# The last expert's down projection in quarters of the output columns, with the second block's first weight chunk between its second and third quarter

## What is computed

```python
xs = jax.vmap(lambda hb, ib: hb[ib])(h, idx)             # 64 tokens per expert
a = jnp.einsum('becd,edf->becf', xs, w_gate)             # 1024 -> 2048
u = jnp.einsum('becd,edf->becf', xs, w_up)
y = jnp.einsum('becf,efd->becd', jax.nn.silu(a) * u, w_down)   # 2048 -> 1024
y = (y * gate[..., None]).astype(h.dtype)
out = jax.ops.segment_sum(y.reshape(-1, dm), seg, num_segments=bn * seq)
...
x = x + out;  x = rms_norm(x, final_g)                   # end of the first block
u = rms_norm_2(h, norm1_gain[l]);  proj = u @ w_in[l]    # start of the second
```

## Time and profile before

| | us |
|---|---|
| median of 3 runs (lowest, highest) | 1888.03 (1887.39, 1888.33) |
| the profiled execution, by the same clock as the runs | 1889.88 |
| its span in the trace | 1888.1 |
| PE busy | 1737.5 (92%) |
| DVE busy | 668.1 (35%) |
| ACT busy | 443.6 (23%) |
| 16 DMA engines, share of the span | 64.5% |

### The profile page before, as it was taken

The page is one execution under the profiler, slowest core; times in us unless marked ns, Lnnn a source line. Parts: engine busy times, 40 slices in busy tenths (PEclk is TensorE's granted clock), DMA queues, the critical chain, the costliest instruction groups (busy, mean ns, idle before and its releaser), DMA issues. The chain is left out here.

```text
span 1888.1 us, 19429 instructions
## 1 busy us (share of the span) xinstructions
PE 1737.5 (92%) x8120; PEld 1038.7 (55%) x8120; DVE 668.1 (35%) x903; ACT 443.6 (23%) x546; POOL 0.2 (0%) x4
## 2 busy tenths in 40 slices
PE   6999996999897997979979799799999999999997
PEld 5888874343342432324323243257767788888885
DVE  7886533101010010101101001057645475645654
ACT  4534322110010100101000010065333343423332
POOL 0000000000000000000000000000000000000000
PEclk9999997999999999999999999999999999999999
DMA  5235436999999999999999999950402223222311
GB/s 183 82 91 174 161 140 250 400 428 428 427 428 428 430 428 428 428 429 428 429 428 428 428 427 428 427 195 1 178 27 87 88 89 112 89 89 89 111 45 44
DMA packets 76389, 492.47 MB, mean 261 GB/s; under 512 B 7472, under 2 KB 12592, under 8 KB 51504
## 3 DMA queue, kind: packets, MB, share of 16 engines
q1 hardware_dynamic: 76336, 491.71, 64.5%
HBM read 487.49 MB, written 2.10 MB: 259 GB/s over the span
## 5 line engine op out<-in xcount | busy, mean ns | idle before, releaser
L1182 PE MATMUL ps<-xs,xe 128*64 128x512 f32 x2048 | 461.5, 598 | 66.6 <-DMA xs<-w_up 35.3
L1182 PEld LDWEIGHTS ps<-xs,xe 128*64 128x64 f32 x2048 | 141.7, 137 | 379.1 <-issue 264.6
L1194 PE MATMUL ps<-xs,hidT 128*64 128x512 f32 x1024 | 229.8, 596 | 13.9 <-DMA xs<-w_down 9.2
L412 DVE TENSOR_TENSOR lo<-raw,hi 128x2048 fp32r<-128x2048 f32 (+1 forms) x73 | 164.8, 2258 | 174.6 <-ACT hi L403 171.4
L1409 DVE TENSOR_TENSOR hid<-hid,ps 128x512 f32<-128x512 f32 x32 | 20.6, 684 | 524.1 <-PE ps L1182 524.1
L403 ACT ACTIVATE hi<-raw 128x2048 fp32r<-128x2048 f32 (+1 forms) x73 | 138.0, 1890 | 218.5 <-PE ps L466 98.5
L466 PE MATMUL ps<-xh,hi 128*128 128x512 f32 x416 | 165.2, 397 | 0.8 <-DVE ga L931 0.8
L466 PE MATMUL ps<-xl,hi 128*128 128x512 f32 x416 | 162.2, 390 | 0.0
L1194 PEld LDWEIGHTS ps<-xs,hidT 128*64 128x64 f32 x1024 | 73.9, 136 | 148.2 <-issue 127.1
L442 PE MATMUL ps<-xh,hi 128*128 128x512 f32 x384 | 150.2, 391 | 1.1 <-DVE xt L1915 0.9
L442 PE MATMUL ps<-xl,hi 128*128 128x512 f32 x384 | 149.4, 389 | 0.0
(11 more groups left out here) (415 smaller groups left out, 1782.4 us busy)
## 6 DMA issues: line engine op xcount, KB each, us to landing
xs<-w_up SPq DMA_DIRECT2D x64, 2048.0 KB, 32.8
xs<-w_gate SPq DMA_DIRECT2D x64, 2048.0 KB, 32.0
xs<-w_down SPq DMA_DIRECT2D x64, 2048.0 KB, 31.3
raw<-w_in SPq DMA_DIRECT2D x25, 1024.0 KB, 6.7
raw<-ffn_up_w SPq DMA_DIRECT2D x24, 1024.0 KB, 5.1
raw<-ffn_down_w SPq DMA_DIRECT2D x12, 1024.0 KB, 5.1
raw<-w_out SPq DMA_DIRECT2D x8, 1024.0 KB, 5.0
xin<-x_t SPq DMA_DIRECT2D x4, 512.0 KB, 8.0
```

Source lines behind the costliest of these rows:

```text
L412: dve.tensor_tensor(lo[slot][:, 0:size], raw[:, raw_slot(n), 0:size], hi[slot][:, 0:size].bitcast(F32), ALU.subtract).then_inc(sem("lo_don ...
L1182: mm = pe.matmul(ps[64 * half:64 * half + 64, bank + b, :], xe[:, k, CAP * u:CAP * (u + 1)], xs[n % NXS][:, f:f + 512], start=(k == 0), st ...
L1194: mm = pe.matmul(ps[64 * nn:64 * nn + 64, YB, :], hidT[:, 4 * (c % 2) + kk, CAP * half:CAP * (half + 1)], xs[n % NXS][:, kk * D + nn * 512 ...
```

## The change

The host lays out the last expert's `w_down` a second time, as `w_down_q`: quarter q holds all 2048 rows and the columns 256q to 256q+255. It is still 2 MB a quarter. The last expert's down projection then runs quarter by quarter (`down_by_columns`): 32 matmuls of 128x64 by 128 columns each, into banks 4 and 7 in turn. After each quarter ACT copies 256 columns of `yy`, so two tiles of `xt` can be scattered (`last_scatter`, through two banks instead of three). PE's order becomes: quarters 0 and 1, tiles 0 to 3 scattered, chunk N2 multiplied, quarters 2 and 3, tiles 4 to 7 scattered, sums of squares, chunk N2+1. SP issues chunk N2's load ahead of quarters 2 and 3. ACT and DVE follow: the work on tiles 0 to 3 comes before that on tiles 4 to 7, and DVE now makes `lo` of chunk N2 behind the first four adds and `lo` of N2+1 behind all eight low parts. Quarters 2 and 3 have new places in memory, since `xh` and `xl` of tiles 0 to 3 are now written before they are used; `ivc` and `cur` move for the same reason.

```diff
+        "w_down_q": i["w_down"][0][NE - 1].reshape(4, P, 4, 4, 256).transpose(1, 3, 0, 2, 4).reshape(P, 4, XCH),
...
-        ivc = at("ivc", [P, 2, NE], F32, B + 60.5)
-        cur = at("cur", [P, 2, 2], F32, B + 60.75)
+        ivc = at("ivc", [P, 2, NE], F32, B + 55.5)
+        cur = at("cur", [P, 2, 2], F32, B + 55.75)
...
+        x67 = at("x67", [P, 2, XCH], F32, 64)
+        xq3 = at("xq3", [P, XCH], F32, B + 73)
+        last_home = (xs[4][:], xs[5][:], x67[:, :, XCH // 2:], xq3[:])
...
+            def down_by_columns(i):
+                pe.wait_ge(sem("hidT_done"), i * 4 + 4)
+                for q in range(4):
+                    n = NX - 4 + q
+                    x_arrived(pe, n, 0)
+                    if q >= 2:
+                        pe.wait_ge(sem("yy_done"), YLAST + 2 * (q - 1))
+                    home = last_home[q]
+                    for c in range(4):
+                        for kk in range(4):
+                            f = 256 * (4 * c + kk)
+                            for nn in range(2):
...
+                                mm = pe.matmul(ps[64 * nn:64 * nn + 64, last_bank(q), 0:P],
+                                               hidT[:, 4 * (c % 2) + kk, CAP * (c // 2):CAP * (c // 2 + 1)], wv,
+                                               start=(c == 0 and kk == 0), stop=(c == 3 and kk == 3))
+                    mm.then_inc(sem("xs_used"), 1)
+                    if q == 1:
+                        last_scatter(0)
+                        last_scatter(1)
+                        chunk_mms(pe, N2, PP, 0, 4, xh, xl, closes=False, by_tile=("xl_done", KD + 1))
+                last_scatter(2)
+                last_scatter(3)
+            def last_scatter(q):
+                if q == 0:
+                    pe.wait_ge(sem("t1_done"), NE // 2 + 1)
+                pe.wait_ge(sem("yy_done"), YLAST + 2 * (q + 1))
+                for m in (2 * q, 2 * q + 1):
+                    if m >= 2:
+                        pe.wait_ge(sem("sc_taken"), KD * (NE // 2) + m)
+                    pe.matmul(ps[:, TB + m % 2, :], yy[:, m * P:(m + 1) * P], t1[:], start=True, stop=True) \
+                        .then_inc(sem("sc_ps"), 1)
...
-                        act.wait_ge(sem("xs_used"), NX - 4)
-                        make_hi(act, NEXP)
+                        for q in range(4):
+                            act.wait_ge(sem("xs_used"), NX - 3 + q)
+                            for nn in range(2):
+                                o = 64 * nn
+                                a(yy[64:P, 256 * q + 128 * nn:256 * q + 128 * nn + 128], ps[o:o + 64, last_bank(q), 0:P], ACT.Copy,
+                                  scale=cur[o:o + 64, 1, 1:2]).then_inc(sem("yy_done"), 1)
+                            if q == 1:
+                                make_hi(act, NEXP)
+                                for m in range(4):
+                                    new_tile(act, m)
+                        break
...
+            for m in range(4):
+                add_last(m)
             make_lo(dve, NEXP)
...
+            for m in range(4):
+                new_rest(m)
+            for m in range(4, KD):
+                add_last(m)
+            for m in range(4, KD):
+                new_rest(m)
             make_lo(dve, NEXP + 1)
...
-            chunk_mms(pe, N2, PP, 0, 4, xh, xl, closes=False, by_tile=("xl_done", KD + 1))
...
+            for m in range(4, KD):
+                new_tile(act, m)
+                if m == 5:
                     make_hi(act, NEXP + 1)
...
-            for n in range(NX - 16, NX):
+            for n in range(NX - 16, NX - 4):
                 load_x(n)
-            for j in range(4):
+            for q in range(4):
+                n = NX - 4 + q
+                if q == 2:
+                    sp.wait_ge(sem("xs_used"), NX - NXS + NEXP % NRAW // 2 + 1)
+                    load_chunk(sp, NEXP)
+                sp.wait_ge(sem("xs_used"), min(n - NXS + 1, NX - NXS) if q < 2 else NX - NXS)
+                src = w["w_down_q"][:, q, :]
+                d(last_home[q], src.rearrange("p (a b) -> p a b", a=2) if q == 2 else src).then_inc(x_sem(n % NXS), 16)
+            for j in range(1, 4):
```

More of the change, by code:

```diff
@@ L1160, in rest_of_indices, with last_bank @@
             mm.then_inc(sem("idb_ps"), 1)
+        YLAST = 4 * (NE // 2 - 1) + 3
+        def last_bank(q):
+            return (YB, TB + 2)[q % 2]
         def experts_pe(pe):
@@ L1224, in pair @@
                     pe.wait_ge(sem("yy_done"), i * 4 + (2 * u + 1))
+                    if u == 1 and last:
+                        down_by_columns(i)
+                        break
                     for c in range(4):
@@ L1235, in pair @@
                                 gather(pe, k)
+            def down_by_columns(i):
[10 more added lines that the diff above has]
+                            for nn in range(2):
+                                wv = home[:, f // 2048, f % 2048 + 128 * nn:f % 2048 + 128 * nn + 128] if q == 2 else \
+                                    home[:, f + 128 * nn:f + 128 * nn + 128]
+                                mm = pe.matmul(ps[64 * nn:64 * nn + 64, last_bank(q), 0:P],
[17 more added lines that the diff above has]
+                        .then_inc(sem("sc_ps"), 1)
             pair(0, first=True)
@@ L1240, in experts_pe @@
             pair(NE // 2 - 1, last=True)
-            for q in range(4):
-                scatter(pe, NE // 2, q)
         def experts_act(act, a):
@@ L1414, in experts_dve, with new_rest, add_last, new_tile @@
             pair(NE // 2 - 1, last=True)
-            make_lo(dve, NEXP)
[L1416 to L1424, removed]
+            stt = dve.scalar_tensor_tensor
+            def new_rest(m):
+                dve.wait_ge(sem("xh_done"), KD + m + 1)
+                stt(xl[:, m, :], xt[:, m, :], gxx[:, m:m + 1], xh[:, m, :].bitcast(F32), ALU.mult, ALU.subtract) \
+                    .then_inc(sem("xl_done"), 1)
+            def add_last(m):
+                dve.wait_ge(sem("sc_ps"), KD * (NE // 2) + m + 1)
+                tt(xt[:, m, :], xt[:, m, :], ps[:, TB + m % 2, :], ALU.add).then_inc(sem("sc_taken"), 1)
+            for m in range(4):
+                add_last(m)
+            make_lo(dve, NEXP)
+            for m in range(4):
[4 more added lines that the diff above has]
+                new_rest(m)
             make_lo(dve, NEXP + 1)
         N2, SCS = NEXP, 1 + KD * (NE // 2 + 1)
+        def new_tile(act, m):
+            act.wait_ge(sem("sc_taken"), SCS - KD + m + 1)
+            act.activation(xh[:, m, :], xt[:, m, :], ACT.Copy, scale=gxx[:, m:m + 1]).then_inc(sem("xh_done"), 1)
+            for j, g in enumerate((None, gss)):
+                act.activation(squared(j, m), xt[:, m, :], ACT.Square, scale=1.0 if g is None else g[:, m:m + 1]) \
+                    .then_inc(sem("nrm_sq"), 1)
         def squared(j, k):
@@ L1433, in second_pe @@
         def second_pe(pe):
-            chunk_mms(pe, N2, PP, 0, 4, xh, xl, closes=False, by_tile=("xl_done", KD + 1))
-            pe.wait_ge(sem("yy_done"), 4 * (NE // 2) + 1)
+            pe.wait_ge(sem("yy_done"), YLAST + 8)
             for k in range(KD):
@@ L1602, in second_act @@
         def second_act(act, a):
-            for m in range(KD):
-                if m == 4:
+            for m in range(4, KD):
+                new_tile(act, m)
+                if m == 5:
                     make_hi(act, NEXP + 1)
[L1607 to L1611, removed]
             make_hi(act, N2 + 2)
```

## The result

The changed kernel takes 1891.07 us (median of 20 runs, 1887.74 to 1893.98) against 1888.52 for the kernel before in the same session (1885.57 to 1890.59): ratio 1.0013, 95% interval [1.0007, 1.0019], so +2.5 us, between +1.3 and +3.6. By the bound of the prediction, 0.2%, that is the same; forecast were +2.2 us and 1890.2. The profiled execution has a span of 1892.1 us, 4.0 more than the one before, and the traces say where these 4.0 are.

The account below looks back on a forecast made before the run. PE's lost time at the handover from waiting for weights to unbroken work bounds the gain: losses of 9.0 us (0.6, 3.9, 2.2, 0.4, 1.9) against 6.9 before give +2.2 us, 1890.2, range 1886.0 to 1895.0.

Parts of the forecast that it names:

- the side of it: Whole kernel: less than 0.2%, 3.8 us, counts as the same; chances same 0.70, slower 0.25, faster 0.05.
- Quarters: Last expert's down projection on PE: each quarter of 32 matmuls costs 3.7 us, as a down chunk did.
- The rival by which weight loads bind them at 68 ns: Quarters on PE: 68.5 ns an instruction, 4.4 us a quarter, in all +5.0 us, 1893.0; chance 0.12.
- Arrivals: Weight stream: loads land in order of issue, quarter 1 at 1220.1, chunk N2 at 1222.8, quarter 2 at 1227.7.
- The banks: Scatters on PE: two banks for three make the third matmul wait for the first add, 0.2 us a group.
- The pause: PE ahead of chunk N2: waits 3.9 us for DVE's lo subtraction (2.2) and first low part (0.75).
- The clock: Chunk N2 on PE: starts at 1.2 GHz behind the pause for 3.3 to 5.6 us, losing 2.2 us (1.6 to 2.8).
- The tail: Ahead of chunk N2+1: ACT limits, then DVE's lo part comes last; PE starts at 1264.9, losing 1.9 us.
- Behind it: After the start of N2+1: SP's next loads come 8 us later and the root moves to about 1270; both covered.
- the longer stall at 1418 us: PE's 4.4 us pause at 1417 to 1421.4: half clock behind it lasting 3.3 or at least 5.6 us.
- A real gain needs the pause and the tail both gone: Handover, rival of a gain over 3.8 us: needs 3.9 + 2.2 + 2 gone; an error in my favour 0.03.

Follow-up runs that it names:

- e2: The changed kernel with PE taking quarter 2 ahead of chunk N2 instead of behind it; ratio 0.9977 to the kernel before.
- e4: The changed kernel with DVE making four low parts ahead of chunk N2's lo part, and PE multiplying all of the hi part first; ratio 0.9983 to the kernel before.
- e5: The changed kernel with four scatter matmuls repeated, their result unused, in PE's pause ahead of chunk N2; ratio 0.9996 to the kernel before.
- e7: The changed kernel run again without any edit; ratio 1.0005 to the kernel before.
- e1: The changed kernel with hi and lo of chunk N2+1 made under chunk N2, ahead of tiles 4 to 7; ratio 0.9994 to the kernel before.
- e3: The changed kernel with quarter 2 ahead of chunk N2, and hi and lo of N2+1 made ahead of tiles 4 to 7; 1883.66 us, ratio 0.9972 to before.
- e6: The changed kernel with chunk N2 loaded and multiplied behind all quarters, ACT's and DVE's order following; ratio 0.9982 to the kernel before.
- e8: e6 with DVE's lo part of chunk N2 moved behind the adds of tiles 4 and 5; ratio 0.9982 to the kernel before.

## Why the prediction was right

The value (+2.2, measured +2.5 [+1.3, +3.6]) and the side of it were right. That the value came so close is in part luck: by the prediction's own yardstick, the start of chunk N2+1, the change cost 1.45 us and not 2.2, and the rest of the median's +2.5 came from no term of the sum. A clock loss behind L1548 in some executions, 1.71 us each, would be enough; that it is this isn't shown. The mechanism was right step by step, counted from the transposes (0.79 subtracted from the trace after):

- **Quarters.** Forecast 3.7 us each, from the row of the same form; measured 3.57 (two in 7.14), 56 ns an instruction. The rival by which weight loads bind them at 68 ns falls. The Trainium skill ("TensorE: Matmul & The Clock Gate", Back-to-back issue gap) has 81 ns per matmul at 128 columns; the traces don't agree with it for 128x64 loads in the two halves of the array.
- **Arrivals.** Quarter 0 started at 1216.80 (forecast 1216.8), quarter 1 without a wait. That chunk N2 lands ahead of quarter 2 is shown by ACT, which starts on it at 1225.61 right behind its copies; in e2, with the same loads, ACT starts on the chunk at 1223.96, and PE waits for quarter 2 until 1227.42.
- **The banks.** Forecast 0.2 us for each group of scatters; between DVE's second and third add it is 0.25 (1226.75 to 1227.86, where 0.86 is the usual spacing). The sum given for it, 0.86 + 0.2 + 0.69 against 2 x 0.86, makes only 0.03: it leaves out the way from the add back to PE. The second group took 3.88 us, forecast 3.7.
- **The pause.** Forecast 3.9 us for DVE's subtraction and the first low part, measured 3.74; e4 shows 2.21 of it to be the subtraction.
- **The clock.** Forecast 2.2 (1.6 to 2.8), measured 1.71 in the trace and 1.64 in e5. I had averaged two stretches; the price was at the lower one in all three profiles with this pause (changed, e7, e1).
- **The tail.** Forecast 1.9 us, ACT first and DVE's lo part last; measured 1.84 (1264.97 less 1256.13 + 7.0), and 1.85 taken away by e1. The start of N2+1 was forecast for 1264.9 and came at 1264.18 on the scale of before; 0.5 us of the difference are the clock's and 0.5 the faster quarters'; longer steps between them, the scatters above all, took 0.3 back.
- **Behind it.** From N2+1 to the wait ahead of L1548 both kernels take the same: 97.0 us (1262.73 to 1359.74, and 1264.97 to 1361.93). The later loads of SP (1268.99 instead of 1260.96, 8 us as forecast) cost nothing.

What the prediction lacks is the clock at a place that it didn't name. It gave the longer stall at 1418 us a spread and passed over the shorter wait ahead of L1548, which cost 1.71 us in both profiles of the changed kernel. "A real gain needs the pause and the tail both gone" held by the traces (e2 alone -3.32 us, e3 -5.49, where over 3.8 was asked), though the runs of e2, -4.3 us (-6.0 to -2.5), don't decide it; but it was written as if nothing short of an error could bring that; one line in PE's order and two in ACT's and DVE's did.

## What to carry to other kernels

When work is moved forward to fill an engine's wait, look at what every other engine has queued ahead of the first thing the moved work needs: here the waits for weights and for ACT were gone, and one 2.3 us subtraction in DVE's queue made up 2.2 of the 3.7 us of pause that came in their place; the half clock made the pause dearer by nearly half. Fill a pause on PE with whatever is ready (quarter 2 was there but for 0.4 us), and make the operands of the next chunks while the engines that make them are idle, not between the pieces that PE is waiting for.

## What was not expected of the hardware

- From the handover to the stall of the earlier trace rows a stretch at half clock cost 1.7 or 3.4 us and nothing between, in all eleven profiles (1.71 behind the pause of 3.74 us in three of three; behind the stall of 4.4 us, where PE waits for DVE's `ml`, 3.41 in nine and 1.71 in e6 and e8).
- The clock can step down after PE has gone back to work: in the changed kernel PE restarts at 1232.42, the stretch 1232 to 1233 still has 1.00, and the next 0.59.
- A wait of 1.8 us cost as much clock as one of 3.7 us in four of eleven profiles and none in the other seven; one of 1.75 us (e6), one of 1.53 us (e4) and one of 1.06 us (e8) cost none. Four matmuls without use removed the loss in e5.
